# Block 2's attention: forget sums carried as extra rows of the query and key tiles, and HGRN's output on VectorE in three parts

## What is computed

```python
# forgetting attention: 8 heads of 64, blocks of 128 queries
logf = log_sigmoid(f_logit + f_bias)
c = cumsum(logf, axis=1)                         # per head, over positions
s = einsum('bhtd,bhsd->bhts', qh[t0:t1], kh[:t1]) * scale
s = s + c[t0:t1, None] - c[None, :t1]            # masked causally
pr = softmax(s);  o = pr @ vh
# end of HGRN2: o (4 heads of 128) normalised per head, times silu(g)
o = rms_norm(o, o_gain);  o = o * silu(g)
```

## Time and profile before

| | |
|---|---|
| median of 3 runs | 1187.66 us (1186.81 to 1190.53) |
| profiled execution, its own time | 1187.62 us |
| its span | 1185.7 us |
| TensorE matmuls busy | 1142.7 us (96%) |
| VectorE busy | 481.2 us (41%) |
| ScalarE busy | 410.5 us (35%) |
| GpSimd busy | 221.2 us (19%) |
| HBM traffic over the span | 279 GB/s |

### The profile page before, as it was taken

One profiled execution on the slowest core, in us unless ns is written; L12 is line 12 of the kernel. 1 busy time (PEld: TensorE's weight loads), 2 busy tenths in 40 slices (PEclk: granted clock), 3 DMA queues, 4 the chain that ended last, 5 costly groups with the idle time before them and its releaser, 6 DMA issues.

```text
span 1185.7 us, 15608 instructions
## 1 busy us (share of the span) xinstructions
PE 1142.7 (96%) x5930; PEld 761.2 (64%) x5930; DVE 481.2 (41%) x971; ACT 410.5 (35%) x609; POOL 221.2 (19%) x100
## 2 busy tenths in 40 slices
PE   4999999999999999999999998999999999999997
PEld 1678867775444444444544435978877788888886
DVE  2475552753222222222222215788444662333236
ACT  3534453332121111111112106664244364444334
POOL 0163323300000000000000003101214354433522
PEclk9899999999999999999999999999999999999999
DMA  9896366689999999999999995644224464654541
GB/s 355 327 327 258 126 251 222 268 332 383 401 423 423 423 423 423 422 424 423 422 423 422 421 420 197 212 144 143 71 72 142 151 213 148 207 163 180 190 167 47
DMA packets 92634, 331.69 MB, mean 280 GB/s; under 512 B 4241, under 2 KB 27058, under 8 KB 66978
## 3 DMA queue, kind: packets, MB, share of 16 engines
q1 hardware_dynamic: 91952, 330.36, 71.9%
q0 software_dynamic: 432, 0.48, 0.2%
q10 hardware_dynamic: 194, 0.06, 0.0%
HBM read 329.84 MB, written 1.05 MB: 279 GB/s over the span
## 4 chain that ended last, share of the span: by engine, by line
PE 82%; DMA 7%; DVE 6%; issue 2%; ACT 2%; SPq 0%; DVEq 0%; ACTq 0%
PE ps L1218 17%; PE ps L860 14%; PE ps L861 13%; PE ps L862 13%; PE ps L1261 8%; DMA ring<-in_w 5%; PE ps L1189 2%; DMA ring<-in_w_ada 2%; PE ps L1190 2%; DVE ring_r L2013 1%; PE ps L933 1%; PE ps L1275 1%; ACT ring_r L1571 1%; PE ps L1370 1%; PE ps L1276 1%
## 5 line engine op out<-in xcount | busy, mean ns | idle before, releaser
L835 POOL TENSOR_TENSOR ring_r<-ring,ring_r 128x1024 fp32r<-128x1024 f32 x76 | 197.0, 2612 | 476.4 <-ACT ring_r L1571 476.3
L861 PE MATMUL ps<-ring_r,hl_r 128*128 128x512 f32 x528 | 211.0, 400 | 0.0
L860 PE MATMUL ps<-ring_r,hl_r 128*128 128x512 f32 x480 | 197.3, 411 | 10.6 <-DVE hr_r L2106 6.2
L1218 PE MATMUL ps<-ring,arena 128*64 128x512 f32 x896 | 199.3, 594 | 0.9 <-DMA ring<-in_w 0.8
L862 PE MATMUL ps<-ring_r,hr_r 128*128 128x512 f32 x480 | 191.9, 400 | 0.0
L1571 ACT ACTIVATE ring_r<-ring 128x2048 fp32r<-128x2048 f32 x90 | 167.4, 1906 | 64.3 <-PE ps L862 44.1
L2013 DVE TENSOR_TENSOR ring_r<-ring,ring_r 128x2048 fp32r<-128x2048 f32 x52 | 121.3, 2339 | 84.3 <-ACT ring_r L1571 84.1
L1218 PEld LDWEIGHTS ps<-ring,arena 128*64 128x64 f32 x896 | 62.7, 137 | 120.4 <-issue 114.9
L860 PEld LDWEIGHTS ps<-ring_r,hl_r 128*128 128x128 f32 x480 | 91.7, 191 | 41.0 <-issue 14.6
L861 PEld LDWEIGHTS ps<-ring_r,hl_r 128*128 128x128 f32 x528 | 100.9, 191 | 21.9
L862 PEld LDWEIGHTS ps<-ring_r,hr_r 128*128 128x128 f32 x480 | 91.6, 191 | 22.3
(11 more groups left out here) (370 smaller groups left out, 1832.0 us busy)
## 6 DMA issues: line engine op xcount, KB each, us to landing
ring<-in_w SPq DMA_DIRECT2D x72, 2048.0 KB, 19.7
ring<-in_w_in SPq DMA_DIRECT2D x21, 2048.0 KB, 8.0
ring<-in_w_ada SPq DMA_DIRECT2D x16, 1024.0 KB, 10.3
...
```

The source lines that it names most:

```text
L835: nc.gpsimd.tensor_tensor(rest[:, a:b], w[:, a:b], lead[:, a:b].bitcast(F32), ALU.subtract).then_inc(sem("w_rest_b"), 1)
L860: mm(o, lhsT=a_lead, rhs=b_lead, start=start, stop=False, skip_group_check=True)
L861: mm(o, lhsT=a_lead, rhs=b_rest, start=False, stop=False, skip_group_check=True)
L1218: last = mm(H[slots_of(e), :], lhsT=xs[:, k, slots_of(e)], rhs=w, start=k == 0, stop=k == KD - 1)
```

## The change

The scores of a head become one product over 128 rows. Two tiles of 8 heads, q8 and k8, hold the 64 dimensions of a head in one half of the partitions (`with_dims`) and the free half (`with_bias`) for the forget sums. GpSimd fills the query's free half with one row of ones per head and zeros. `forget_sums` computes the sums of all heads once, behind unit hi1, from a zero-padded tile of gates in cpad (two small VectorE instructions in place of one), and ScalarE copies them into the free half of k8. A head's scores are then two matmuls, of 128 and 256 columns. Since q8 covers the rows of qrow and krow, the queries are transposed behind hg1 in place of fk1, and the copies out of PSUM are of half the partitions, four for each of q and k in place of two. The tile KE[0] of the levels moves to a part of the gates.

On VectorE, `values_rest` of a step moves behind its maximum and normalisation. `hgrn_rows` of iteration 2 is cut: gated rows in iteration 2, factors in 3, scaled rows in 4. `hgrn_rests` stays in iteration 7 but stands last in it. In numbers of matmuls, 56 of 128 columns become 8 of 128 and 8 of 256, and 3 more for the sums.

```diff
@@ -231,6 +231,8 @@
         xbT = part(20, 4).rearrange("p (c t) -> p c t", t=T)
+        q8 = part(0, 8).rearrange("p (h t) -> p h t", t=T)
+        k8 = part(12, 8).rearrange("p (h t) -> p h t", t=T)
         ga1b = part(0, 4)
@@ -282,10 +284,20 @@
         QE = [G16[:, 4 * n:4 * n + 4, :] for n in range(2)]
-        KE = [part(0, 4).rearrange("p (h t) -> p h t", t=T),
+        KE = [G16[:, 8:12, :],
               ring[:, SCRATCH, 8 * T:12 * T].rearrange("p (h t) -> p h t", t=T)]
...
         sg = ga2b[:, :].rearrange("p (t c) -> p t c", t=TT)
+        forget = cpad[:, :, :].rearrange("p (t k) m -> p t (k m)", t=TT)
+        def with_bias(t8, odd):
+            return t8[0:DH, 1:HEADS:2, :] if odd else t8[DH:P, 0:HEADS:2, :]
+        def with_dims(t8, u, odd):
+            h = 4 * u + odd
+            return t8[odd * DH:odd * DH + DH, h:h + 3:2, :]
         scT = ybT_flat.rearrange("p (n t) -> p n t", t=P)
@@ -371,12 +383,14 @@
                 small_order += ["rsb", "fox"]
-            if name == "fk1":
-                small_order += ["tq_b0", "tq_b1"]
             if name in LEVEL_AT:
...
                 small_order += ["tk_b0", "tk_b1"]
+            if name == "hi1":
+                small_order.append("foxc")
+            if name == "hg1":
+                small_order += ["tq_b0", "tq_b1"]
             if name == "gate_b11":
@@ -418,7 +432,7 @@
                 dense_released[f"ffn{m}{t}"] = sem("arow_ready"), TT * m + t + 1
-        small_released = {"cT": (sem("c_ready"), 1), "params": (sem("pcol_ready"), 1), "rsb": (sem("rsb_ready"), 1),
+        small_released = {"foxc": (sem("kT_ready"), 4), "cT": (sem("c_ready"), 1), "params": (sem("pcol_ready"), 1), "rsb": (sem("rsb_ready"), 1),
                           "fox": (sem("fox_z"), TT), "foxr": (sem("fox_rows"), 1), "ppt": (sem("pt_rest"), 1)}
@@ -431,9 +445,10 @@
             small_released[f"yt{u}"] = sem("hy_rest"), u + 1
-            for tag in ("", "_b"):
-                small_released[f"tq{tag}{u}"] = sem("qT_ready"), u + 1 + 2 * SECOND[tag]
-                small_released[f"tk{tag}{u}"] = sem("kT_ready"), u + 1 + 2 * SECOND[tag]
+            small_released[f"tq{u}"] = sem("qT_ready"), u + 1
+            small_released[f"tk{u}"] = sem("kT_ready"), u + 1
+            small_released[f"tq_b{u}"] = sem("qT_ready"), 2 * u + 4
+            small_released[f"tk_b{u}"] = sem("kT_ready"), 2 * u + 6
         for n, group in enumerate(("g2", "g3")):
@@ -840,8 +855,17 @@
             pool.wait_ge(sem("moe_ys1_done"), PAIRS - 1)
-            nc.gpsimd.memset(scT, 0.0).then_inc(sem("scores_zeroed"), 1)
+            nc.gpsimd.memset(cpad[:, :, :], 0.0).then_inc(sem("pool_filled"), 1)
+            nc.gpsimd.memset(scT, 0.0).then_inc(sem("pool_filled"), 1)
             for m in range(M["fq"], M["pproj"]):
+                if m == M["gate_b1"]:
+                    small.ready(pool, "tq_b1")
+                    for odd in range(2):
+                        rows = slice(DH - odd * DH, P - odd * DH)
+                        pick = ident[rows, rows.start:rows.start + HEADS // 2]
+                        nc.gpsimd.tensor_copy(with_bias(q8, odd), pick.unsqueeze(2).to_broadcast([DH, HEADS // 2, T])
+                                              ).then_inc(sem("pool_filled"), 1)
+                        pool.wait_ge(sem("pool_filled"), 3 + odd)
                 rest_weights(m)
@@ -984,22 +1008,26 @@
                 o = small.claim(pe, f"qk{tag}{h}")
-                pe.wait_ge(sem("qT_ready"), h // 4 + 1 + 2 * SECOND[tag])
-                pe.wait_ge(sem("kT_ready"), h // 4 + 1 + 2 * SECOND[tag])
-                a = DH * (h % 2)
                 if SECOND[tag]:
-                    pe.wait_ge(sem("fox_c_ready"), 1)
-                    first, second = (fz[:, 0, t * HEADS + h:t * HEADS + h + 1].to_broadcast([P, P]) for t in range(TT))
-                    for n, (t, s) in enumerate(((0, 0), (1, 0), (1, 1))):
-                        into = o[:, n * P:(n + 1) * P]
-                        mm(into, lhsT=qT[a:a + DH, h // 2, t * P:(t + 1) * P], rhs=kT[a:a + DH, h // 2, s * P:(s + 1) * P],
-                           start=True, stop=False)
-                        mm(into, lhsT=first, rhs=ones if s else upto, start=False, stop=s == 0)
-                    mm(o[:, 2 * P:SC], lhsT=second, rhs=upto, start=False, stop=True).then_inc(small.done, 1)
-                    return
-                mm(o[:, 0:P], lhsT=qT[a:a + DH, h // 2, 0:P], rhs=kT[a:a + DH, h // 2, 0:P], start=True, stop=True)
-                mm(o[:, P:SC], lhsT=qT[a:a + DH, h // 2, P:T], rhs=kT[a:a + DH, h // 2, :], start=True,
-                   stop=True).then_inc(small.done, 1)
+                    pe.wait_ge(sem("pool_filled"), 4)
+                    pe.wait_ge(sem("qT_ready"), 2 * (h // 4) + 4)
+                    pe.wait_ge(sem("kT_ready"), 2 * (h // 4) + 6)
+                    q, k = q8[:, h, :], k8[:, h, :]
+                else:
+                    pe.wait_ge(sem("qT_ready"), h // 4 + 1)
+                    pe.wait_ge(sem("kT_ready"), h // 4 + 1)
+                    a = DH * (h % 2)
+                    q, k = qT[a:a + DH, h // 2, :], kT[a:a + DH, h // 2, :]
+                mm(o[:, 0:P], lhsT=q[:, 0:P], rhs=k[:, 0:P], start=True, stop=True)
+                mm(o[:, P:SC], lhsT=q[:, P:T], rhs=k, start=True, stop=True).then_inc(small.done, 1)
+            def forget_sums():
+                o = small.claim(pe, "foxc")
+                pe.wait_ge(sem("fox_c_ready"), 2)
+                mm(o[:, 0:P], lhsT=forget[:, 0, :], rhs=upto, start=True, stop=True)
+                mm(o[:, P:T], lhsT=forget[:, 0, :], rhs=ones, start=True, stop=False)
+                mm(o[:, P:T], lhsT=forget[:, 1, :], rhs=upto, start=False, stop=True).then_inc(small.done, 1)
@@ -1410,12 +1438,14 @@
                     fox_gate_columns()
-                if name == "fk1":
-                    head_transposes("tq_b", qrow, "q_normed", 2)
                 if name in LEVEL_AT:
                     level(level_names[LEVEL_AT[name]])
+                if name == "hi1":
+                    forget_sums()
                 if name == "hg0":
                     head_transposes("tk_b", krow, "k_normed", 2)
+                if name == "hg1":
+                    head_transposes("tq_b", qrow, "q_normed", 2)
                 if name == "gate_b11":
@@ -1560,6 +1590,9 @@
                 return t[:, 2 * u:2 * u + 2, :]
+            def pair(src):
+                return src.rearrange("p (j t) -> p j t", t=T)
@@ -1768,6 +1801,12 @@
                 af(E[n % 2], E[n % 2], ACT.Exp).then_inc(sem("decay_ready"), 1)
+            def heads_out(t8, name, ready):
+                for u in range(2):
+                    src = small.ready(act_, f"{name}{u}")
+                    for odd in range(2):
+                        af(with_dims(t8, u, odd), pair(src)[odd * DH:odd * DH + DH, :, :], ACT.Copy).then_inc(sem(ready), 1)
@@ -1815,14 +1854,21 @@
                 if unit == "fk1":
-                    for i in range(2):
-                        copy_out(two_tiles(qT, i), small, f"tq_b{i}", "qT_ready")
                     decay(0)
+                if unit == "hi1":
+                    src = small.ready(act_, "foxc")
+                    for odd in range(2):
+                        into = with_bias(k8, odd)
+                        rows = slice(DH - odd * DH, P - odd * DH)
+                        af(into, src[rows, 0:T].unsqueeze(1).to_broadcast([DH, HEADS // 2, T]), ACT.Copy
+                           ).then_inc(sem("kT_ready"), 1)
                 if unit in LEVEL_AT and LEVEL_AT[unit] + 1 < len(level_names) - 1:
...
                 if unit == "hg0":
-                    for i in range(2):
-                        copy_out(two_tiles(kT, i), small, f"tk_b{i}", "kT_ready")
+                    heads_out(k8, "tk_b", "kT_ready")
+                if unit == "hg1":
+                    small.ready(act_, "tq_b1")
+                    heads_out(q8, "tq_b", "qT_ready")
                 if unit == "gate_b11":
@@ -2380,7 +2426,12 @@
             link(v.tensor_tensor(fz[:, 0, :], fz[:, 0, :], fz[:, 2, :], ALU.subtract))
-            v.tensor_scalar(fz[:, 0, :], fz[:, 0, :], -1.0 / SCALE, None, ALU.mult).then_inc(sem("fox_c_ready"), 1)
+            dve.wait_ge(sem("pool_filled"), 1)
+            by_pair = fz[:, 0, :].rearrange("p (t i two) -> p t i two", t=TT, two=2)
+            for odd in range(2):
+                at = DH - odd * DH
+                v.tensor_scalar(forget[:, :, at:at + HEADS // 2], by_pair[:, :, :, odd], -1.0 / SCALE, None,
+                                ALU.mult).then_inc(sem("fox_c_ready"), 1)
@@ -2475,7 +2526,7 @@
-            dve.wait_ge(sem("scores_zeroed"), 1)
+            dve.wait_ge(sem("pool_filled"), 2)
             n_levels = len(level_names)
@@ -2493,18 +2544,24 @@
-            def hgrn_rows():
+            def hgrn_gated_rows():
...
```

(16 more changed lines are left out.)

## The result

| | before | after |
|---|---|---|
| median of the runs | 1187.63 us (1186.81 to 1190.53, 4 runs) | 1179.33 us (1177.8 to 1180.02, 4 runs) |
| profiled execution, its own time | 1187.62 us | 1180.02 us |
| its span | 1185.7 us | 1178.2 us |

The ratio is 0.9921, with a 95% interval of 0.9908 to 0.9934: the kernel is 8.3 us faster. The forecast was 1175.8 us, in a range of 1172.4 to 1180.0. The result lies in the range, 3.5 us above the forecast.

The account below looks back on a forecast made before the run. The prediction took TensorE's list of instructions to bound block 2's attention; -16.5 + 1.6 + 0.2 + 2.85 = -11.85 us against the profiled 1187.62 us gave 1175.8 us, range 1172.4 to 1180.0.

Parts of the forecast that it names:

- Part 1: Block 2's attention scores on TensorE: 0.65 us per head instead of 2.72, over 8 heads -16.5 us.
- Part 2: HGRN levels: forget sums and moved query transposes give TensorE more work, +1.6 us, bounds 0.7 and 3.5.
- Part 3: Softmax steps: VectorE keeps up with the shorter steps; +0.2 us for ScalarE's closest claim, bounds 0 and 1.
- Part 4: Step 7: claim of pt_b5 waits for VectorE's rest of values 3, then pv_b4 for HGRN's rest; +2.85 us.
- The rival of the falling clock: TensorE's clock falls after the wait of step 7, costing 1.7 us more, 1177.5 us; chance 0.14.
- The clock of 1.00 throughout 840 to 900: Expected sign in TensorE's timeline: granted clock stays at full 2.4 GHz from 840 to 900 us.
- the missing wait: Rival: no new TensorE wait at step 7, giving 1172.9 us; chance 0.15.
- the old price of the pairs: Rival: score matmul pairs still cost 0.42 and 0.52 us, gain only 14.2, giving 1178.1 us; chance 0.08.
- late levels: Rival: ScalarE's 4.2 us more push an HGRN level's decay past TensorE's need, +2 us, 1177.8 us; chance 0.04.
- steps paced by softmax: Rival: VectorE's softmax loop takes 6.84 us every step, scores' gain returns as waits, 1192.1 us; chance 0.04.

Follow-up runs that it names:

- x4: The kernel before with each head's seven score matmuls sorted by form, three over 64 rows, then four over 128; time alone counts: 1183.44 us.
- x3: The kernel before with only the change's VectorE loop (HGRN output in three parts, rests last), seven matmuls per head kept: 1195.23 us.
- x2: The changed kernel with VectorE's loop of before: rests ahead of each maximum, all HGRN rows in iteration 2: 1181.25 us.
- x1: The changed kernel with the rest of values and the HGRN rests put ahead of the maximum in iteration 7 only: 1173.09 us, again 1174.06.
- x6: The changed kernel with five matmuls of 256 columns, results unused, where TensorE waits 2.40 us in step 7: 1178.22 us.
- x8: x1 with GpSimd's rests of gate_b3 held back until VectorE has normalised head 5: 1173.91 us.

## Why the prediction was right, and where it was off

By its own steps, against the forecast of -11.85:

- **Part 1, -16.5: right.** 0.66 us per head; from head to head the distance is 2.05 to 2.07 us less in five places, and 1.95 in the one behind the wait of step 6. x4 shows why: the dear part was the change of form.
- **Part 2, +1.6: right.** First level's products to the first score 58.76 us in after (843.61) and 57.38 in before (840.45): +1.38; from the projection's start (725.93 and 724.20) it is +1.43. The old place of the transposes gave most of its time back as a longer wait (1.14 for 0.51), and the second wait hardly changed (0.57 for 0.56). The copies on ScalarE were dearer than forecast (2.44 for 2.1 each time). The leads of gate_b1 start at 828.67; less the 1.8 us by which this trace is late, that is the forecast 826.8. GpSimd's two bias copies, whose price was left open, took 2.37 us together, ahead of them.
- **Part 3, +0.2: wrong in size and in place.** Measured 0.97, one wait in step 6. The prediction followed the claims with VectorE's durations of before, and moved GpSimd's rests by nothing. But the new loop starts GpSimd's rests earlier, so that work which had met idle time of VectorE met its normalisation; x3 shows the same with steps of the old length, and x2, with short steps and the old loop, has no wait there (GpSimd starts at 872.73 and stretches one instruction, L2030 to 1.78 us). The upper bound of 1 us held it, by luck: it was meant for what ScalarE does.
- **Part 4, +2.85: right.** 2.40 + 0.23 = 2.63 us, by the claim named; x1 removes it.
- **The rival of the falling clock came true on top of the forecast.** It had a chance of 0.14 and a price of 1.7; x6 measures 1.49. The argument against it, that the wait stands in full work, counted for nothing. The clock of 1.00 throughout 840 to 900, which the prediction named as a sign, was not seen. The forecast had the clock at nothing, the high end of the range had room for it.

So -16.5 + 1.4 + 1.0 + 2.6 + 1.5 = -10.0 from measured parts, and -9.33 from level to end. Of the 0.7 between, some 0.4 stand around the waits: from head 5 to head 6 the distance is 5.92 us, 1.13 above the usual 4.79 for a wait of 0.97; from head 6 to head 7 it is 5.76 for 5.65 in x8; and from L1022 to L1036 in step 7 it is 3.00, 2.57 above the usual 0.43 for a wait of 2.40. The rest is not placed. In x8, without the waits of step 6 and the long one, parts and trace agree (-16.5 + 1.4 + 0.4 = -14.7, measured -14.86). The medians differ by 8.3. The 1 us that is missing there lies ahead of the first level: nine traces with the changed levels reach it between 782.66 and 786.38 us, three with the old ones between 781.98 and 783.07. Nearly all of it is there already at the projection's start (723.77 to 729.06 against 723.12 to 724.20). Ahead of that the change adds one instruction, GpSimd's memset of cpad (0.31 us at 690.35), and none of TensorE's waits is put down to it. So this looks like the scatter of executions, but nine against three traces don't settle it.

The other rivals: the missing wait, the old price of the pairs, late levels and steps paced by softmax are all excluded by the rows above. What was nearest to the last was x2, where VectorE did pace two steps.

**The version that beats both** is x1, a loop with the rests ahead of the maximum in iteration 7 alone: 1173.09 and 1174.06 us on two chips, 0.5% under the change. x8 is as fast, and 1.35 us shorter by its trace.
